# Direct high parts, an even mix of modulation units and sums by additions of whole chunks, in a two-block transformer kernel

## The reference

```
# block 1, layer 0: tokens x and context ctx are modulated per channel
sh, sc, g = split(silu(cond) @ ada_w + ada_b, 3)
xm  = x   * (1 + sc_l) + sh_l        # the same for ctx with its own sc, sh
q, k, v, o, z, gates, ... = split(xm @ w_in_even)     # mLSTM, pooling
x = layer_norm(ALPHA * x + g_l * (y @ w_out_even))
# layer 1: a gated unit with a second layer_norm after w_out_odd
# block 2: rmsnorm, retention, gated recurrence, w_mix_out,
#   cross attention to the memory: keys = rmsnorm(mem) @ xa_w_k,
#   rmsnorm, convolutional feed-forward (w_ffn_up, w_ffn_down), rmsnorm
```

## Time and profile before

| | |
|---|---|
| runs, us | 3183.54, 3176.96, 3175.62 (median 3176.96) |
| the profiled execution, us | 3178.01 |
| its span, us | 3176.2 |
| mean granted clock of PE | 0.991 |
| PE busy | 3093.1 us, 97% |
| PE weight loads (beside the matmuls) | 2658.5 us, 84% |
| DVE busy | 2244.8 us, 71% |
| ACT busy | 1633.4 us, 51% |
| POOL busy | 59.5 us, 2% |
| DMA | 666.42 MB, mean 210 GB/s |
| the modulation rows are turned (line 825), from | 172.0 us |

### The profile page before, as it was taken

One profiled execution on the slowest core, in us unless ns is written; L12 is line 12 of the kernel. 1 busy time (PEld: TensorE's weight loads), 2 busy tenths in 40 slices (PEclk: granted clock), 3 DMA queues, 4 the chain that ended last, 5 costly groups with the idle time before them and its releaser, 6 DMA issues.

```text
span 3176.2 us, 45015 instructions
## 1 busy us (share of the span) xinstructions
PE 3093.1 (97%) x16842; PEld 2658.5 (84%) x16842; DVE 2244.8 (71%) x2732; ACT 1633.4 (51%) x1984; POOL 59.5 (2%) x52
## 2 busy tenths in 40 slices
PE   7999999999999999999999999999999999999998
PEld 5787877888788887888888888888888888888887
DVE  6779987788768787655767865567457777777544
ACT  6655444555534566544456655445345555555443
POOL 0002300000000000000000000000000000000000
PEclk8999999999999999999999999999999999999999
DMA  7977784787568664655555555566445555555554
GB/s 293 339 256 270 255 296 172 264 311 239 181 211 289 244 220 159 208 182 183 176 186 175 168 189 194 190 225 198 142 146 181 190 189 188 185 185 196 188 191 139
DMA packets 180248, 666.42 MB, mean 210 GB/s; under 512 B 20084, under 2 KB 20468, under 8 KB 178808
## 3 DMA queue, kind: packets, MB, share of 16 engines
q1 hardware_dynamic: 178424, 660.09, 61.2%
q10 hardware_dynamic: 1664, 4.19, 0.3%
HBM read 657.91 MB, written 6.29 MB: 209 GB/s over the span
## 4 chain that ended last, share of the span: by engine, by line
PE 82%; DVE 10%; DMA 3%; ACT 2%; DVEq 1%; issue 1%; ACTq 0%; SPq 0%
PE acc L760 44%; PE acc L764 22%; DVE w_lo L1980 4%; PE acc L771 3%; PE acc L773 3%; PE acc L772 3%; DMA ada_raw<-in_w_ada 1%; ACT w_hi L1275 1%; DVE mod_raw L1991 1%; DMA mod_raw<-in_w_mod 1%; PE acc L928 1%; PE msc L1170 0%; DMA raw<-in_w_mix_out 0%; PE msc L874 0%; PE msc L1190 0%
## 5 line engine op out<-in xcount | busy, mean ns | idle before, releaser
L1980 DVE TENSOR_TENSOR w_lo<-raw,w_hi 128x1024 fp32r<-128x1024 f32 x1020 | 1242.3, 1228 | 561.2 <-ACT w_hi L1275 551.8
L1275 ACT CAST w_hi<-raw 128x1024 fp32r<-128x1024 f32 x1020 | 1061.8, 1049 | 803.2 <-PE acc L764 556.9
L760 PE MATMUL acc<-a_pair,w_hi 128*128 128x512 f32 x2944 | 931.8, 398 | 9.8 <-DVE w_lo L1980 4.1
L764 PEld LDWEIGHTS acc<-a_pair,w_lo 128*128 128x128 f32 x2944 | 554.0, 188 | 131.0
L764 PE MATMUL acc<-a_pair,w_lo 128*128 128x256 f32 x2944 | 579.3, 278 | 0.0
L760 PE MATMUL acc<-b_pair,w_hi 128*128 128x512 f32 x1792 | 571.0, 400 | 5.9 <-DVE w_lo L1980 5.9
L760 PEld LDWEIGHTS acc<-a_pair,w_hi 128*128 128x128 f32 x2944 | 451.2, 189 | 13.4 <-DVE a_pair L2172 3.7
L760 PE MATMUL acc<-f_pair,w_hi 128*128 128x512 f32 x1408 | 442.4, 395 | 0.0
L764 PEld LDWEIGHTS acc<-b_pair,w_lo 128*128 128x128 f32 x1792 | 338.2, 189 | 80.1
L764 PE MATMUL acc<-b_pair,w_lo 128*128 128x256 f32 x1792 | 353.2, 279 | 0.0
L764 PEld LDWEIGHTS acc<-f_pair,w_lo 128*128 128x128 f32 x1408 | 264.5, 188 | 62.5
(11 more groups left out here) (363 smaller groups left out, 2782.6 us busy)
## 6 DMA issues: line engine op xcount, KB each, us to landing
raw<-in_w_ffn_up SPq DMA_DIRECT2D x176, 512.0 KB, 4.1
mod_raw<-in_w_mod SPq DMA_DIRECT2D x128, 512.0 KB, 5.1
raw<-in_w_ffn_down SPq DMA_DIRECT2D x88, 512.0 KB, 3.3
ada_raw<-in_w_ada SPq DMA_DIRECT2D x64, 512.0 KB, 5.7
raw<-in_w_xa_k SPq DMA_DIRECT2D x32, 512.0 KB, 6.5
raw<-in_w_k SPq DMA_DIRECT2D x32, 512.0 KB, 4.7
raw<-in_w_v SPq DMA_DIRECT2D x32, 512.0 KB, 5.0
raw<-in_w_even_out SPq DMA_DIRECT2D x32, 512.0 KB, 4.6
```

Of the source, the lines that this page charges most:

```text
L760: pe.matmul(acc[:, bank(stage, g) + m, :], w_h[:, cols], pair[:, :, kc, :], start=begin, stop=False, skip_group_check=True)
L764: mm = pe.matmul(acc[:, bank(stage, g) + m, 0:T], w_l[:, cols], pair[:, 0, kc, :], start=False, stop=end, skip_group_check=True)
L1275: nc.scalar.copy(w_hi[:, slot], source).then_inc(hi_done, 1)
L1980: vec.tensor_tensor(w_lo[:, slot], source, w_hi[:, slot].bitcast(F32), ALU.subtract).then_inc(lo_done, 1)
```

## The change

- The 58 "a" units are spread evenly over the 22 "w" units: 2 or 3 behind each, alternating (2.64 in the mean). The stage still has 96 units and the modulation rows are still turned at unit 87.
- In mem_k the memory's first three quarters are turned into the pair in step 0, the fourth in step 1 (ACT) and 2 (DVE). The squares, their sums, the root, the reciprocal, the turn and the copy are at steps named by new constants, later and further apart than before. The context is loaded before load 84 and waits only for the sums.
- ACT makes the high part of the modulated chunks itself from x, with scale and bias (two activations of one chunk), and doesn't wait for DVE's chunks any more; the semaphore chunks_made is gone. DVE computes its chunks, waits for ACT's high part, and subtracts in the same step. The ctx chunks end in step 0 of ctx_k (before: 2), those of x run from step 9 of ctx_v to step 0 of lat_k (before: 8 to 1).
- ctx_k has 2 modulation sums (before 5), lat_o 12 (before 9).
- In mem_vb quarters 2 and 3 come one step sooner on ACT and DVE (only the normalisation of quarters 0 to 2 keeps its place).
- Reduces over a strided view are replaced by additions: four_sums adds chunks 0 and 1 to 2 and 3 (512 columns), then the two halves (256 columns); the mean's sum is three additions of 256 columns, one after the other; in ffn_down one addition of 256 columns. dve.drain() stands between dependent ones.

```diff
--- before.py
+++ after.py
@@ -107,10 +107,8 @@
             mixed, a = a[:first], a[first:]
             for n, w in enumerate(self.kinds):
 
-                take = -(-len(a) // (ADA_OVER - n)) if n < ADA_OVER else 0
-                mixed += [w] + a[:take]
-                a = a[take:]
-            assert not a
+                begin, end = (-(-min(m, ADA_OVER) * len(a) // ADA_OVER) for m in (n, n + 1))
+                mixed += [w] + a[begin:end]
             self.kinds = mixed
         if gate:
 
@@ -197,8 +195,8 @@
     return [(2 * m + 1) * n // (2 * k) for m in range(k)]
 
 
-MOD_AT = {"ctx_k": range(8, 18, 2), "ctx_v": spread(16, 9), "lat_k": spread(18, 13), "lat_v": spread(16, 9),
-          "lat_q": spread(16, 11), "lat_o": spread(16, 9), "pool_u": spread(16, 9), "mlstm_z": spread(16, 13),
+MOD_AT = {"ctx_k": (13, 16), "ctx_v": spread(16, 9), "lat_k": spread(18, 13), "lat_v": spread(16, 9),
+          "lat_q": spread(16, 11), "lat_o": spread(16, 12), "pool_u": spread(16, 9), "mlstm_z": spread(16, 13),
           "pool_z": spread(16, 10), "even_out": range(0, 16, 2), "sgu_u": spread(32, 18), "sgu_z": spread(26, 14)}
 MOD_PLACE = {}
 for _s in STAGES:
@@ -209,6 +207,10 @@
 CTX_AT = STAGE["mem_k"].n - 7
 MOD_TURN = CTX_AT - 2
 LAM_AT = 8
+CTX_LOAD_AT = 84
+MEM_SQUARE_AT = {2: 0, 5: 1, 8: 2, 11: 3}
+MEM_SUM_AT = {7: 0, 10: 1, 13: 2, 15: 3}
+MEM_ROOT_AT, MEM_SCALE_AT, MEM_TURN_AT, MEM_TAKE_AT = 16, 17, 22, 27
 TURN_KEYS_AT = (6, 8)
 CTX_ROWS_AT = 6
 EXP_AT = 9
@@ -225,9 +227,9 @@
 ROW_SUM_AT = 20
 MIX_SUMS_AT = 13
 MIX_NORM_AT = 14
-NORMALISE_AT = {4: 0, 5: 1, 7: 2, 9: 3}
-SQUARES_AT = {5: 0, 6: 1, 8: 2, 10: 3}
-QUARTERS_AT = {6: 0, 8: 1, 10: 2, 11: 3}
+NORMALISE_AT = {4: 0, 5: 1, 7: 2, 8: 3}
+SQUARES_AT = {5: 0, 6: 1, 8: 2, 9: 3}
+QUARTERS_AT = {6: 0, 7: 1, 9: 2, 10: 3}
 ANGLES_AT = 4
 MOD_ISSUE = {}
 _order = [(_s.name, _j) for _s in STAGES for _j in range(_s.n if _s.iters == 1 else 0)]
...
@@ -596,9 +598,9 @@
                 for j, (kind, g, k, _) in enumerate(stage.kinds):
                     if stage.name == "mem_k" and j == ADA_RING:
                         load_mem()
-                    if j == 24:
-
-                        sp.wait_ge(pe_step, AFTER["mem_norm"]["pe"])
+                    if j == CTX_LOAD_AT:
+
+                        sp.wait_ge(pe_step, BEFORE["mem_norm"]["pe"] + 1)
                         nc.sync.dma_start(x[:], t["ctx"]).then_inc(ctx_in, 16)
                     n = PLACE[kind].index((stage.name, j))
                     if n >= RING:
@@ -802,8 +804,8 @@
             steps.end("mem_pair")
 
             def mem_sums(j):
-                q = j - 6
-                if 0 <= q < 4:
+                if j in MEM_SUM_AT:
+                    q = MEM_SUM_AT[j]
                     if q == 0:
                         pe.wait_ge(consts_in, 48)
 
@@ -812,7 +814,7 @@
                         mm = pe.matmul(msc[:, 0, 0:T], ones[:], x[:, c, :], start=(c == 0), stop=(c == DC - 1))
                     if q == 3:
                         steps.done(mm)
-                if j == 13:
+                if j == MEM_TURN_AT:
 
                     steps.wait(dve=1)
                     for tt in range(2):
@@ -1050,7 +1052,7 @@
                     steps.end("ln1")
                 if j == MIX_SUMS_AT:
 
-                    column_sums((3, 5, 7, 8))
+                    column_sums((3, 4, 7, 8))
                     steps.end("mix_norm")
                     steps.end("mix_pair")
 
@@ -1406,8 +1408,7 @@
 
             def mem_chunks(j):
 
-                if j < 4:
-                    q = j
+                for q in (range(3) if j == 0 else range(3, 4) if j == 1 else ()):
                     if q == 0:
                         act.wait_ge(params_in, 16)
                     act.wait_ge(mem_in[q], 16)
@@ -1416,16 +1417,20 @@
                     steps.done(mm)
                     if q == 3:
                         steps.end("mem_pair")
-                if 4 <= j < 8:
-                    q = j - 4
+                if j in MEM_SQUARE_AT:
+                    q = MEM_SQUARE_AT[j]
                     steps.done(nc.scalar.activation(x[:, 4 * q:4 * q + 4, :].rearrange("p a b -> p (a b)"),
                                                     mem[:, 4 * q:4 * q + 4, :].rearrange("p a b -> p (a b)"), ACT.Square))
-                if j == 11:
+                if j == MEM_ROOT_AT:
                     act.wait_ge(eps_set, 1)
                     rms("mem_norm", token_scale)
                     steps.end("mod")
-                if j > CTX_AT:
-                    high(j - CTX_AT - 1, 0)
+                if j >= CTX_AT:
+                    if j == CTX_AT:
+
+                        act.wait_ge(dve_step, AFTER["mod"]["dve"])
+                        act.wait_ge(ctx_in, 16)
+                    high(j - CTX_AT, 0)
 
             def store_keys(i, g):
 
@@ -1454,8 +1459,11 @@
 
             def high(q, n):
 
-                act.wait_ge(chunks_made, 8 * n + q + 1)
-                nc.scalar.copy(a_hi[:, 2 * q:2 * q + 2, :], buf_a[:, 2 * (q % 2):2 * (q % 2) + 2, :]).then_inc(chunks_high, 1)
+                which = 1 - n
+                for c in range(2 * q, 2 * q + 2):
+                    mm = nc.scalar.activation(a_hi[:, c, :], x[:, c, :], ACT.Identity, bias=mod[:, c, which:which + 1],
+                                              scale=mod[:, 16 + c, which:which + 1])
+                mm.then_inc(chunks_high, 1)
 
             run("mem_k", store_keys, side=mem_chunks)
 
@@ -1485,8 +1493,8 @@
                 ran(act.nop())
 
             def wide_and_last(j):
-                if j < 2:
-                    high(6 + j, 0)
+                if j == 0:
+                    high(7, 0)
                 if j == 4:
                     act.wait_ge(wide_in, 16)
                     nc.scalar.activation(cond_wide[:], cond_wide[:], ACT.Silu).then_inc(wide_set, 1)
@@ -1517,6 +1525,8 @@
                 if j > 8:
 
                     act.wait_ge(unit_used, RING + STAGE["ctx_v"].u0 + j)
+                    if j == 9:
+                        act.wait_ge(x_in, 16)
                     high(j - 9, 1)
 
             run("ctx_v", values, side=key_tokens)
@@ -1731,7 +1741,7 @@
                 q = SQUARES_AT.get(j)
                 if q is not None:
 
-                    steps.wait(dve=(1, 2, 4, 6)[q])
+                    steps.wait(dve=(1, 2, 5, 6)[q])
                     buf = buf_a if q % 2 == 0 else buf_c
                     for m in range(4):
                         c = 4 * q + m
@@ -2174,8 +2184,7 @@
 
             def mem_chunks(j):
 
-                if 1 <= j < 5:
-                    q = j - 1
+                for q in (range(3) if j == 0 else range(3, 4) if j == 2 else ()):
                     if q == 0:
                         dve.wait_ge(params_in, 16)
                     dve.wait_ge(mem_in[q], 16)
@@ -2187,11 +2196,11 @@
                             mm.then_inc(pair_ready, 1)
                     if q == 3:
                         steps.end("mem_pair")
-                if j == 12:
+                if j == MEM_SCALE_AT:
 
                     steps.wait(act=5)
                     steps.done(vec.reciprocal(token_scale[:], token_scale[:]))
-                if j == 15:
+                if j == MEM_TAKE_AT:
 
                     steps.wait(pe=2)
                     vec.tensor_copy(mem_scale, msc[:, 0, 0:2 * P:P])
@@ -2248,25 +2257,22 @@
 
             def modulated(q, slab, which, n):
 
-                if 2 <= q < 10:
-                    dve.wait_ge(chunks_high, 8 * n + q - 1)
-                    low(a_hi, a_lo, q - 2)
-                    dve.drain()
-                if q < 8:
-                    for c in range(2 * q, 2 * q + 2):
-                        mm = vec.tensor_scalar(buf_a[:, 2 * (q % 2) + c % 2, :], slab[:, c, :], mod[:, 16 + c, which:which + 1],
-                                               mod[:, c, which:which + 1], ALU.mult, ALU.add)
-                    mm.then_inc(chunks_made, 1)
+                for c in range(2 * q, 2 * q + 2):
+                    vec.tensor_scalar(buf_a[:, 2 * (q % 2) + c % 2, :], slab[:, c, :], mod[:, 16 + c, which:which + 1],
+                                      mod[:, c, which:which + 1], ALU.mult, ALU.add)
+                dve.drain()
+                dve.wait_ge(chunks_high, 8 * n + q + 1)
+                low(a_hi, a_lo, q)
 
             run("mem_k", none(), side=mem_chunks, dest=keys_out, scale=token_scale)
 
             def last_ctx(j):
-                if j < 3:
-                    modulated(7 + j, x, 1, 0)
+                if j == 0:
+                    modulated(7, x, 1, 0)
 
             def last_lat(j):
-                if j < 2:
-                    modulated(8 + j, None, None, 1)
+                if j == 0:
+                    modulated(7, x, 0, 1)
 
             def conv3(first):
 
@@ -2320,10 +2326,10 @@
             def ctx_states(j):
                 if j == CTX_ROWS_AT:
                     ctx_rows()
-                if j >= 8:
```

(31 more changed lines are left out.)

## The result

| | before | changed |
|---|---|---|
| median of the runs, us | 3177.17 (3175.62 to 3183.54) | 3157.05 (3153.06 to 3162.59) |
| ratio, 95% interval | | 0.9931 (0.9917 to 0.9944) |
| the profiled execution, us | 3178.01 | 3159.27 |
| its span, us | 3176.2 | 3157.5 |

A forecast was written before the change was run, and what follows sets the result against it. PE was taken as the bound, busy 3093.1 of 3176.2 us, with its few greatest waits mostly on DVE. Terms of 11.2 + 3.8 + 3.9 + 2.0 + 0.3 + 4.0 = 25.2 us gave a median of 3152, range 3142 to 3165.

The forecast's parts named there:

- the opening: mem_k: reciprocal, pair and squares, even mix and later ctx load together gain 11.2 us.
- (a): Opening (mem_k): a later reciprocal of the memory's norm removes PE's 5.01 us wait and low clock; 6.7 us.
- (b): Opening (mem_k): the memory's pair made earlier and its squares spread; 2.0 us, bounds -1 to 4.
- (c): Opening (mem_k): even mix takes back 4.0 us, later ctx load charged 1.5; net 2.5 us, bounds -4 and 7.
- rival 1: Opening paced by DMA at 345 GB/s whatever the mix; 8.7 us come back, 3161; chance 0.17.
- Direct high parts: ctx_k: last low part moves from step 2 to 0, removing PE's wait and low clock; 3.8 us.
- DVE-bound stretch: ctx_k to lat_k: fewer modulation sums and earlier low part remove waits at 247.27 and 315.06; 3.9 us.
- Sums: Layer norms: additions for reduces shorten PE's waits of 1.74 and 0.67; 2.0 us, plus 0.3 in ffn_down's last reduce.
- mem_vb: Second norm: quarters 2 and 3 one step sooner bring the last quarter sum forward; 4.0 us with clock, bounds -1 and 7.
- Rival 2: More is won: all 7.1 us of 68 to 157 and both mem_vb waits whole; 33.3 us, 3144; chance 0.12.
- 3: Rival: gains come back on DVE or ACT, waits move to the next w_lo; only 5.0 + 1.7 stay, 3170; chance 0.05.
- 4: Rival: DVE and ACT in lockstep in the new pair step, 16 steps cost 26.4 us; slower, 3186; chance 0.03.

The follow-up runs named there:

- both: The changed kernel with ctx issued at load 24 and nine sums in lat_k, thirteen in pool_u: 3150.99 us (0.9908) and 3150.81 us (0.9905).
- again: The changed kernel as it is, run once more in a second group of runs: 3158.96 us, ratio 0.9936.

## Why the prediction came out as it did

**The direction and most of the size were right;** 20.1 us were gained of 25.2. The total is nearer than its terms: the opening gave 3.6 us of its 11.2 (5.1 by the mean turn of 166.9), and from num to v_ret 8.6 came where 6.0 were forecast. That these two misses offset each other is luck. The terms:

- *(a) Reciprocal, 6.7.* The wait of 5.01 and its clock went as forecast, and the number came out: 6.9 timed and 6.2 at the turn, measured with ctx at 24. In part by luck: the forecast has neither the 2.42 us that the reciprocal costs at its new place, nor the 2.26 at 67.92 that goes with the old one, and the two nearly cancel.
- *(b) and (c), pair and mix, 2.0 + 4.0.* With the old norm steps, the even mix and ctx at 24 the turn is at 169.55, 2.5 us before the 172.04 of the kernel before: 2.5 in place of 6.0, from one execution each, where executions of one opening differ by up to 7.6. The old mix alone costs nothing measurable. This is rival 1 at work in part: the queues give 345 GB/s at a share of 0.95 in 68 to 121, and a better order of the same bytes doesn't help. (By its own terms, 5.74 less 5.2 over 17 groups, rival 1's 8.7 us should read 9.2; its 3161 stands.)
- *(c) The later load of ctx, charged 1.5.* The step that failed. The forecast looked at who needs ctx (DVE, at unit 87) and at how fast a lone load lands (8.2 us). It named the last two "a" units as delayed and put no wait on them. But the queues are full when ctx is issued (a share of 0.99 from 140 to 157), and those units' loads come in behind it: PE waits 2.5 to 4.5 us there in all five profiles. Against ctx at 24 that costs 3.9 us at the mean turn and 3.3 and 2.4 in the medians, and the relief hoped for at the front isn't there, since with the norm's wait gone the queues have room where a ctx issued at load 24 lands.
- *Direct high parts, 3.8.* The mechanism was right, wait and clock, and is worth 4.1 in "both", but nothing measurable in the changed kernel.
- *DVE-bound stretch, 3.9.* Both waits went, and the forecast never asked what DVE owes next: thirteen sums in lat_k and the chain of the gates. The wait at the states grew from 0.98 to 3.44 us, with 0.8 to 2.2 us lost behind it, where the granted clock was lower (175.26 and 176.68 us from the states to num, against 174.44). The two terms, 7.7 in sum, gave 8.14 up to the states and lost 0.65 to num (in "again" 6.82 and 2.07). Moving four sums away returns 4.7 us, or 3.8 with ctx at 24.
- *Sums, 2.0 + 0.3, and mem_vb, 4.0.* The sums before mem_va were right, mem_vb was under-estimated. From num to v_ret the changed kernel is 8.6 us faster than before, 2.45 up to mem_va, as the 1.74 and 0.67 of the earlier trace rows promised, and 6.1 behind. The version with reductions has the new steps without the additions: up to mem_va it gains 0.2 us on the kernel before (309.25 against 309.48), behind it 4.0 (694.66 against 698.70). So the steps of mem_vb give 4.0 by themselves and the additions 2.1 to 2.2 more in either stretch, from one execution each. In mem_vb the last quarter sum waits 1.82 us in place of 4.40, unit 12 waits 0.55 in place of 2.12, and unit 11 1.83 in place of 0.74. PE's timeline of the changed kernel:

```profile
1212.95 0.50 PE L773 MATMUL acc<-w_hi,b_pair 128*128 128x512 f32 x1 [1.83 <-DVE w_lo L1990]
1218.11 0.50 PE L773 MATMUL acc<-w_hi,b_pair 128*128 128x512 f32 x1 [0.55 <-DVE w_lo L1990]
1224.29 0.70 PE L783 MATMUL msc<-buf_b,ones 128*128 128x256 f32 x2 [1.82 <-DVE buf_b L2512]
```

By profiles, before to changed: 3.6 to the turn, 8.1 to the states, -0.65 to num, 2.45 to mem_va, 6.1 to v_ret, -0.9 to the end: 18.7. By the rule of the Trainium skill, "VectorE: DVE Perf Modes", section "Rules for kernel authors", that the number of chained operations be kept low, the sums would have given nothing; here two additions of 0.68 and 0.43 us beat one reduction of 2.00, so the measurement decides against that rule taken alone. The same table calls tensor_reduce the slowest DVE operation and advises to restructure it, and this case agrees: 2.00 us for 1024 columns, where w_lo's tensor_tensor of 1024 columns takes 1.23.

Two of the prediction's signs of being wrong came, casts held by their loads in the opening and a wait behind ctx; of its signs of being right the turn near 161 did not. Rival 2 (3144) didn't come, nor 3 or 4: PE is busy 24.00 of 24.00 us from 186 to 210, so ACT inside the pair step was covered. Not tried, so open: the share of the squares' spread within the 6.9 us, the additions of mem_vb at its old steps, and why the opening differs by 7.6 us between executions.

## What to carry to other kernels

Before a large load is moved, read the DMA share of the stretch where it lands, not only when its reader needs it: 2 MB were free where the share was 0.59, and cost 2.4 to 3.9 us where it was 0.99. When a wait goes, follow the engine that it was put down to until its next deadline: a gain of 4.1 us vanished in the gates' chain some 110 us later and came back once four DVE instructions of 1.22 us were moved to a stage where nothing waits for them. Price a version against a second run of itself before its profile is read to a microsecond.

## What the runs showed of the hardware

- A 2 MB load took 8.1 us to land when issued at 47.9 us, with the queues at 0.94 and 366 GB/s with it, and 12.6 us when issued at 145.8, at 1.00 and 392 GB/s.
- Behind a 3.26 us wait of PE came a granted clock of 0.66 over 315 to 325 us, that is the 1.2 GHz level for part of it; with a wait of 0.69 us it was 1.00. A wait of 2.22 us at 203 had 0.66 over the 5 us behind it, and one of 2.42 near 58 us had 1.00: the length of the wait alone doesn't say whether the clock falls.
- DVE takes 2.00 us for a strided reduction of 1024 columns to 256, and 1.18 us from the start of the first to the end of the second for two plain additions that give the same sum (1202.86 to 1204.04 us in mem_vb).
